# Two query tiles fed chunk by chunk, their low parts made by VectorE alone

## The reference, cut to what matters

```python
def rmsnorm(x, g, eps=EPS):
    y = xf * lax.rsqrt(jnp.mean(xf * xf, -1, keepdims=True) + eps)
    return (y * g.astype(jnp.float32)).astype(x.dtype)

def adaln(x, g, shift, scale):
    return rmsnorm(x, g) * (1 + scale) + shift

def mixer_cd(h, w_in, w_out, ...):
    z = h @ w_in
    r_p, k_p, v_p, q, kd, vd = jnp.split(z, [...], axis=-1)
    yc, s_f, s_b = rwkv_time_mix(h, r_p, k_p, v_p, ...)   # also reads h and its neighbours in time
    q = rmsnorm(q.reshape(bsz, n, D_HEADS, HEAD_DIM), q_g)
    kd = rmsnorm(kd.reshape(bsz, n, D_KV_HEADS, HEAD_DIM), k_g)
...
```

## Time and profile before

| what | value |
|---|---|
| median of 3 runs | 1885.24 us (1884.21, 1885.24, 1885.87) |
| the profiled execution, own time | 1881.16 us |
| its span, first to last instruction | 1879.4 us |
| busy PE, PEld, DVE, ACT, POOL | 94%, 86%, 55%, 42%, 35% of the span |
| chain that ended last | PE 79%, DVE 10%, issue 5%, ACT 3%, POOL 1% |

### The profile page before, as it was taken

One profiled execution on the slowest core, in us unless ns is written; L12 is line 12 of the kernel. 1 busy time (PEld: TensorE's weight loads), 2 busy tenths in 40 slices (PEclk: granted clock), 3 DMA queues, 4 the chain that ended last, 5 costly groups with the idle time before them and its releaser, 6 DMA issues.

```text
span 1879.4 us, 44239 instructions
## 1 busy us (share of the span) xinstructions
PE 1775.3 (94%) x18240; PEld 1620.8 (86%) x18240; DVE 1034.0 (55%) x1846; ACT 792.7 (42%) x1316; POOL 656.5 (35%) x368
## 2 busy tenths in 40 slices
PE   4999999999999999899999799988899999999996
PEld 3865799999999999878888677777799999999996
DVE  6599755443134544893757768776454451154413
ACT  4211445553135543524745455554345541255521
POOL 2300144444334444402112334333544443344442
PEclk8999899999999999899999999999899999999998
DMA  9675531222222221112011000000122222121221
GB/s 379 258 277 223 184 135 68 78 78 78 69 72 73 78 79 67 64 40 73 30 42 63 3 4 4 4 4 4 59 71 75 70 90 79 56 78 67 91 77 56
DMA packets 35348, 159.71 MB, mean 85 GB/s; under 512 B 3936, under 2 KB 4448, under 8 KB 28560
## 3 DMA queue, kind: packets, MB, share of 16 engines
q1 hardware_dynamic: 32832, 152.02, 22.2%
q10 hardware_dynamic: 1872, 3.61, 0.5%
q0 software_dynamic: 512, 2.13, 0.3%
HBM read 154.73 MB, written 3.01 MB: 84 GB/s over the span
## 4 chain that ended last, share of the span: by engine, by line
PE 79%; DVE 10%; issue 5%; ACT 3%; POOL 1%; DVEq 1%; DMA 0%; SPq 0%; PEldq 0%; POOLq 0%; PEld 0%; ACTq 0%
PE ps L220 18%; PE ps L222 18%; PE ps L221 18%; PE ps L2150 4%; PE ps L2095 2%; PE ps L2185 2%; PE ps L814 2%; PE ps L2136 1%; PE ps L1357 1%; PE ps L1647 1%; PE ps L1648 1%; PE ps L1649 1%; PE ps L2116 1%; DVE arena L996 1%; DVE rs L613 1%
## 5 line engine op out<-in xcount | busy, mean ns | idle before, releaser
L259 POOL TENSOR_TENSOR w_lo<-wslot,w_hi 128x1024 fp32r<-128x1024 f32 x130 | 314.1, 2416 | 651.8 <-ACT w_hi L254 648.2
L220 PE MATMUL ps<-xa_hi,w_hi 128*128 128x322 f32 (+1 forms) x1440 | 446.1, 310 | 0.0
L222 PE MATMUL ps<-xa_hi,w_lo 128*128 128x322 f32 (+1 forms) x1440 | 445.9, 310 | 0.0
L221 PE MATMUL ps<-xa_lo,w_hi 128*128 128x322 f32 (+1 forms) x1440 | 445.0, 309 | 0.0
L254 ACT ACTIVATE w_hi<-wslot 128x1024 fp32r<-128x1024 f32 x130 | 138.1, 1063 | 333.8 <-PE ps L222 289.1
L220 PEld LDWEIGHTS ps<-xa_hi,w_hi 128*128 128x128 f32 x1440 | 271.8, 189 | 0.2
L221 PEld LDWEIGHTS ps<-xa_lo,w_hi 128*128 128x128 f32 x1440 | 271.3, 188 | 0.2
L222 PEld LDWEIGHTS ps<-xa_hi,w_lo 128*128 128x128 f32 x1440 | 271.1, 188 | 0.0
L220 PE MATMUL ps<-hid_hi,d_hi 128*128 128x320 f32 x704 | 217.9, 310 | 3.9 <-POOL hid_lo L1234 3.9
L222 PE MATMUL ps<-hid_hi,d_lo 128*128 128x320 f32 x704 | 216.1, 307 | 0.0
L221 PE MATMUL ps<-hid_lo,d_hi 128*128 128x320 f32 x704 | 215.6, 306 | 0.0
(11 more groups left out here) (251 smaller groups left out, 3454.7 us busy)
## 6 DMA issues: line engine op xcount, KB each, us to landing
arena<-in_mod_w SPq DMA_DIRECT2D x48, 1024.0 KB, 7.3
wslot<-in_ffn_up SPq DMA_DIRECT2D x88, 512.0 KB, 3.5
wslot<-in_ffn_down SPq DMA_DIRECT2D x32, 704.0 KB, 4.0
wslot<-in_cd_w SPq DMA_DIRECT2D x22, 512.0 KB, 3.5
wslot<-in_w_out SPq DMA_DIRECT2D x16, 512.0 KB, 3.5
wslot<-in_ab_w SPq DMA_DIRECT2D x12, 512.0 KB, 8.6
x<-in_x_fm SPq DMA_DIRECT2D x2, 1280.0 KB, 7.8
out_y<-arena ACTq DMA_DIRECT2D x8, 320.0 KB, 2.4
```

The lines of the kernel that those rows point to most:

```text
L220: nc.tensor.matmul(out, wh[:, m], hi[:, kk, t], start=(kk == first), stop=False)
L221: nc.tensor.matmul(out, wh[:, m], lo[:, kk, t], start=False, stop=False)
L222: last = nc.tensor.matmul(out, wl[:, m], hi[:, kk, t], start=False, stop=(kk == (k_all - 1 if end is None else end)))
L259: pool.tensor_tensor(wl[:, :], wslot[:, s, 0:tile_cols[base]], wh[:, :], ALU.subtract).then_inc(lo_ready, 1)
```

## The change

What it does: VectorE adds the shift of chunks 0, 3 and 6 itself (`SHIFT_DVE`; a wait for its own result, then two TENSOR_SCALAR), and ACT of the five others; ACT still copies all eight high parts. VectorE makes all eight low parts, each two chunks behind `scaled_h`; POOL makes none. The second `scaled_key` moves up from the end of the chunks to behind chunk 1. ACT makes tile 3's high part behind chunk 0 instead of behind chunk 5. PE takes tiles 2 and 3 together: chunk k of tile 2, then chunk k - 1 of tile 3; the last chunk of tile 3 comes behind `key_sums(0)`. The counts that other waits compare with follow.

```diff
@@ def cd_pe
-            take_parts(pe, base, 1, 0)
             for kk in range(KD):
+                if kk < 2:
+                    take_parts(pe, base, 1, kk)
                 chunk_of_h(pe, 1)(kk)
                 last = product_of_parts(base, 0, [kk], KD, h1_hi, h1_lo)
-            last.then_inc(product, 1)
+                if kk == KD - 1:
+                    last.then_inc(product, 1)
+                if kk:
+                    product_of_parts(base, 1, [kk - 1], KD, h1_hi, h1_lo)
             key_sums(0)
-            tile(3)
+            product_of_parts(base, 1, [KD - 1], KD, h1_hi, h1_lo).then_inc(product, 1)
             key_sums(1)
@@ def cd_act
+                if k in SHIFT_ACT:
...
+                else:
+                    act.wait_ge(h_dve, len(BY_DVE) + SHIFT_DVE.index(k) + 1)
                 nc.scalar.activation(h1_hi[:, k, :], h[:, k, :], ACT.Copy).then_inc(src_hi, 1)
...
                 shifted_h(k)
-                if k == 5:
+                if k == 0:
                     tile_hi(act, base, 1, 1)
@@ def cd_dve
-                last.then_inc(xn_ready, 1)
+                if k in SHIFT_ACT:
+                    last.then_inc(xn_ready, 1)
+                    return
+                st(last)
+                st.wait()
+                for a, b, v in GROUPS:
+                    last = nc.vector.tensor_scalar(h[:, k, a:b], h[:, k, a:b], mods[1][:, k, v:v + 1], None, ALU.add)
+                last.then_inc(h_dve, 1)
...
                 scaled_h(k)
-                if k == 1:
-                    scaled_key(0)
-            source_lo(dve, "dve", 2 * KD, h, h1_hi, h1_lo, range(BY_POOL, KD))
-            scaled_key(1)
+                if k < 2:
+                    scaled_key(k)
+                if k > 1:
+                    source_lo(dve, "dve", 2 * KD, h, h1_hi, h1_lo, [k - 2])
+            source_lo(dve, "dve", 2 * KD, h, h1_hi, h1_lo, range(KD - 2, KD))
@@ def cd_pool
             tile_lo(pool, cd["qk"], 1, 0)
-            source_lo(pool, "pool", 2 * KD, h, h1_hi, h1_lo, range(BY_POOL))
             tile_lo(pool, cd["qk"], 1, 1)
```

More of the change, by code:

```diff
@@ L622, in chunk_of_h @@
         def chunk_of_h(pe, turn):
-            before = (KD - BY_POOL + KD) * turn
             def chunk(kk):
-                if kk < BY_POOL:
-                    pe.wait_ge(src_lo["pool"], BY_POOL * turn + kk + 1)
+                if turn:
+                    pe.wait_ge(src_lo["dve"], KD - BY_POOL + KD + kk + 1)
+                elif kk < BY_POOL:
+                    pe.wait_ge(src_lo["pool"], kk + 1)
                 else:
-                    pe.wait_ge(src_lo["dve"], before + kk - BY_POOL + 1)
+                    pe.wait_ge(src_lo["dve"], kk - BY_POOL + 1)
             return chunk
@@ L646, in chunk @@
                 if kk < KD - 1:
-                    pe.wait_ge(src_lo["pool"], 2 * BY_POOL + kk + 1)
+                    pe.wait_ge(src_lo["pool"], BY_POOL + kk + 1)
                 else:
-                    pe.wait_ge(src_lo["dve"], 2 * (KD - BY_POOL) + KD + 1)
+                    pe.wait_ge(src_lo["dve"], KD - BY_POOL + 2 * KD + 1)
             return chunk
@@ L1314, in head_sums @@
             return last
+        SHIFT_DVE = (0, 3, 6)
+        SHIFT_ACT = tuple(k for k in range(KD) if k not in SHIFT_DVE)
         def cd_pe(pe):
@@ L1416, in shifted_h @@
                 mod = mods[1]
[L1417 to L1421, removed]
+                if k in SHIFT_ACT:
+                    at = len(BY_ACT) + SHIFT_ACT.index(k) + 1
+                    act.wait_ge(xn_ready, at)
+                    for a, b, v in GROUPS:
+                        last = nc.scalar.activation(h[:, k, a:b], h[:, k, a:b], ACT.Identity, bias=mod[:, k, v:v + 1])
+                    last.then_inc(h_act, 1)
+                    act.wait_ge(h_act, at)
+                else:
+                    act.wait_ge(h_dve, len(BY_DVE) + SHIFT_DVE.index(k) + 1)
                 nc.scalar.activation(h1_hi[:, k, :], h[:, k, :], ACT.Copy).then_inc(src_hi, 1)
```

## The result

The changed kernel takes 1890.38 us (median of 6 runs, 1887.23 to 1893.11) where the kernel before, on the same chip, takes 1884.75 (6 runs, 1884.21 to 1885.87): a ratio of 1.0027, with a 95% interval of 1.0016 to 1.0037. The profiled execution took 1889.33 us.

The account below looks back on a forecast made before the run. PE was taken as the bound except where it waits, with DVE's list ending the stage last. Tile 4's start +4.2 and clock +1.8, less 1.5 slack and up to 1 in `turned`, gave +4.1 on 1885.24: 1889.3 us, range 1885.2 to 1892.0.

Parts of the forecast that it names:

- DVE's walk: DVE up to L1477: time freed from POOL is spent on low parts and shifts; +0.4 us, start about 789.6.
- The first chunk: PE before tile 2's first chunk from `h`: stands 4.9 us instead of 1.05 and loses its clock.
- PE 3 us ahead, and the meeting: Second `key_sums` ends 3 us earlier; POOL's tile 4 request falls into L1542 and waits its whole rest, 3.2 us.
- the sum for the stage: End of `turned(0)` at 825.8 to 826.8 against 822.26: +3.5 to +4.5 us, taken as +4.1.
- Tile 4's start: On PE, tile 4 starts at 804.2 where it started at 800.0: +4.2 us.
- the restart at half clock: PE from tile 4 on: about 4 us at half clock after standing 7 us, costing 1.8 us, bounds 1.5 and 3.1.
- The slack of 1.50: PE's wait for DVE at `turned(1)`: PE may come up to 1.5 us later at no cost; all used up.
- the whole shift arrives at the end: Behind `turned(1)` the rest hangs on PE, so all +4.1 us of the stage reach the total time.
- Not held back: Rival at tile 4's low part: POOL does not wait for L1542; +0.5 to +1.5 us; chance 0.26.
- the clock costs more: Rival on PE: half clock nearly 7 us at tile 4 and through `turned` into `lora`; +5.5 to +6.5 us; chance 0.15.
- main case: POOL held back at tile 4, whole shift reaching the end: +2.5 to +5 us, 1887.7 to 1890.3; chance 0.50.
- DVE runs free: Rival: both `w_lo` miss DVE's two-input work, norms end 3.8 us early; 1881.4 to 1883 us; chance 0.09.

Follow-up runs that it names:

- e2: Changed kernel with PE's old order, tile 2 whole and then tile 3: 1885.84 us, ratio 1.0007 to the kernel before.
- e8: Changed kernel with the first low part of `h` right behind the second key, ahead of chunk 2's scaling: 1889.48 us, ratio 1.0021 to the kernel before.
- e1: Changed kernel with the 5.49 us DVE instruction that makes dh cut into eight pieces: 1885.17 us, ratio 0.9995 to the kernel before.
- e7: Changed kernel with DVE's two key norms ahead of the eight `mixed`, nothing else: 1889.63 us, ratio 1.0023 to the kernel before.
- e4: Changed kernel once more, unedited: 1888.45 us, ratio 1.0019 to the kernel before.
- e9: Changed kernel with tile 4's high part ahead of `key_root(0)`, key norms ahead of `mixed`, first low part of `h` behind the second key: 1878.64 us, ratio 0.9967.
- e6: Kernel before, with only DVE's two key norms put ahead of the eight `mixed`: 1885.98 us, ratio 1.0003 to the kernel before.
- e3: Changed kernel with ACT making tile 4's high part ahead of `key_root(0)` and `evict(2)`: 1887.06 us, ratio 1.0013 to the kernel before.
- e5: Changed kernel with tile 4's high part ahead of `key_root(0)` on ACT and DVE's two key norms ahead of `mixed`: 1879.69 us, ratio 0.9965.

## Why the prediction came out as it did

- **DVE's walk: right.** Freed time is spent again. L1477's instruction was put 0.4 us later and started at the same place: a shift's pair takes 0.68, and waits 0.035 for its own result, where I had taken 0.80 and 0.11; three of them make 0.6 us less.
- **The first chunk: right.** At 14.75 where 14.7 was forecast, after 5.01 us where 4.9 was; clock lost behind it. e2 and e8 show what I had not said clearly: that hole is harmless. In e2 it stands and the loss is gone; in e8 the first chunk comes 3.1 us earlier and PE waits for the second, which comes no earlier.
- **PE 3 us ahead, and the meeting: right.** The lead of 3 us is that of the second `key_sums` (33.14 against 36.34); at the first, on which POOL's request hangs, PE is 3.1 us behind the kernel before, as the forecast had it too. First `key_sums` at 31.18 (31.5 forecast), the long instruction at 33.33 (33.8), POOL's request at 35.56 (36.0), and it waited the whole rest: 5.46 against about 5.6. The Trainium skill, page "SBUF — State Buffer", section "Who interferes with whom", says that a VectorE instruction with two SBUF inputs contends with a GpSimd instruction that reads SBUF, and that one with at most one SBUF input does not, if it runs outside the modes that take both ports. The traces agree on both sides: with the two-input instruction cut or not there (e1, e2) POOL takes 2.58 and 2.45; in e7 tile 5's low part, beside the norm's one-input reciprocal, takes 2.37 of the group's 7.71. In which mode the small copy ran that waited 2.40 us in the earlier trace rows no run shows.
- **The size: the sum for the stage was too large.** +4.1 was forecast, +2.83 measured. Tile 4's start was put 4.2 us later and came 3.9 later (37.17 to 41.07; the forecast had put its start of before at 800.0, where the row has 799.80). From there to `turned(0)` the way grew by 1.27 us, from 18.91 to 20.18, where the restart at half clock had been put at 1.8; it lasted 3.6 us, which by the forecast's own working, 3.6 x (1 - 0.146/0.26), makes 1.6. `turned(0)` and `turned(1)` took 3.29 together, not 4.13 as in the earlier trace rows: 0.84 back, where I had counted about 0.4 between nothing and 1. The slack of 1.50 went as forecast. 3.90 + 1.27 - 0.84 - 1.50 = 2.83. So each of three terms, tile 4's start, the restart and `turned`, was 0.3 to 0.5 us too dear, and all three erred the same way.
- **The time: nearer to the forecast than the stage, in part by luck.** 1890.38 us was measured where 1889.3 was forecast. The medians differ by 5.6 us in the first measurement, 3.3 in e4's, and the stage explains 2.8 of either. The rest is not from a step of mine, and it filled up what the sum for the stage had too much. From `lora` to the end, with the same code in all kernels (but that some of the `mixed` reach into it where the norms go first), the profiles have 1055.2 (before), 1058.5 (changed), and 1059.6, 1054.9, 1059.8, 1059.2, 1057.9, 1063.6, 1059.2, 1063.2 and 1057.0 (e1 to e9). One profile is one execution; these lengths don't go with any part of the change that I can name (e6, whose code differs from before only by the place of the norms, has the longest). It may be why e3 and e6 shortened the stage by 3.0 and 1.8 us where the medians show 1.4 and nothing; the 8.9 us of e5 arrive whole (-5.8 against +3.3). So my step "the whole shift arrives at the end" is shown for e5's 8.9 us and not for shifts of 2 or 3. Between 1057 and 1310 us the idle time of PE that grew most is that ahead of the matmuls on L2168 (L2150 before) for which the profile shows no releaser: 14.5 us in the changed kernel, 11.5 before. What makes the small waits longer or shorter stays open.
- **The rivals.** *Not held back* fell by 5.46; *the clock costs more* fell at 3.6 us of half clock behind the hole, though the time, between that rival's 1891.3 and the main case's 1890.3, could not have told the two apart; *DVE runs free* needed tile 4's request ahead of the long instruction and got it only in e2, e3, e5 and e9; of these only e5 and e9, with the norms moved as well, became faster.

## What to carry to other kernels

When a change shifts one engine's requests by a few microseconds, look up what stands on the other engine at the new arrival time: here PE ended tile 2 later, by 3.1 us, so as to end tile 3 earlier, by 3.2, and the first of these brought POOL's request from between small copies into a 5.5 us instruction, and cost more than it gave. Cut a bulk instruction, or put the request ahead of it, where another engine's critical work shares the resource (e1 and e3, each a few lines). And before valuing a lead, ask what ends next: PE's lead paid (0.35%) only when the list that it then waits for was put in the order of its readers (e5). How much of that is due to taking two tiles together is not shown: e2's order of PE with the norms first was not run. PE comes to `turned(0)` at 56.08 before, 55.17 in e2 and 53.57 in e5, so an estimate from these is 1.6 us of the 2.5.

## What was unexpected of the hardware

- Which engine gets in when both are queued differs. POOL waited out the long instruction, then went ahead of the `mixed` queued behind it (802.28 in e3, 800.21 after), and in the changed kernel `mixed` came in between tile 4's and tile 5's subtraction: the latter took 2.95 us instead of 2.4.
- A shift's result is ready for the next DVE instruction 0.035 us later, hardly a wait.
- The granted clock fell to 0.50 while the 30 matmuls of 128x2 ahead of `turned`, or `turned` itself, ran, in ten of the eleven profiles, and in nine of these PE had not stood over 0.3 us there. In e5 it stayed at 1.00, which was worth 2.1 us against the kernel before.
- The length of the untouched 1055 us behind the stage varied by 8.7 us (1054.9 to 1063.6) over eleven profiles of kernels with the same code there (but for some of the `mixed`), more than the whole change is worth in its stage. The 35 runs of the kernel before on one chip lay between 1879.92 and 1890.27 us. A change of 3 us is better judged by events inside the stage, counted from a common one, than by the total.
